# Key pace, softmax start, value pages and norm groups at other block numbers in a hybrid decoder layer

## What is computed

```python
h = rmsnorm(x); proj = h @ w_in                       # 2048 -> 13344 columns
q, k, v, z, xbc, dt, g_attn, g_ssm = split(proj)
attn = moba_attention(q, k, v)      # 16 heads of 64; own block of 256 and the best 3 past ones
ssm  = mamba2(z, xbc, dt)           # conv of width 4, SSD in chunks of 128, grouped RMS norm
merged = sigmoid(g_attn) * (attn @ w_attn_out) + sigmoid(g_ssm) * (ssm @ w_ssm_out)
x = x + rmsnorm(merged @ w_out)
x = x + rmsnorm(swiglu(rmsnorm(x)))                   # 2048 -> 5632 -> 2048
```

## Time and profile before

| | |
|---|---|
| median of three runs | 1809.43 us |
| profiled execution | 1807.29 us, span 1805.5 |
| mean granted TensorE clock | 0.995 of full |
| PE / VectorE / ScalarE / GpSimd busy | 99% / 66% / 51% / 12% |
| VectorE busy, 350 to 420 us | 65.6 of 70 us |
| VectorE busy, 690 to 760 us | 54.0 of 70 us |

### The profile page before, as it was taken

How to read it: one execution, slowest core, us unless ns; L and a number is a source line. 1 busy time by engine, 2 the same in 40 slices (tenths; PEclk the granted TensorE clock), 3 DMA queues, 4 the chain that set the end, 5 groups by cost and what they waited for, 6 DMA issues and landing times.

```text
span 1805.5 us, 35392 instructions
## 1 busy us (share of the span) xinstructions
PE 1782.1 (99%) x14613; PEld 1719.1 (95%) x14613; DVE 1195.2 (66%) x1666; ACT 918.3 (51%) x1737; POOL 216.2 (12%) x127
## 2 busy tenths in 40 slices
PE   8999999999999999999999999999999999999997
PEld 8999999998988988889999899999999999999997
DVE  6478999999887557745744666666666666444443
ACT  5544556554766557533444655554545454444342
POOL 2145644564000000000000000000000000000000
PEclk9999999999999999999999999999999999999998
DMA  8589987897789999695564387767777775655552
GB/s 253 177 272 330 320 265 261 278 305 235 222 281 317 303 295 344 217 304 177 180 223 155 116 281 221 225 226 231 230 217 232 229 235 182 216 176 170 175 180 80
DMA packets 397810, 421.40 MB, mean 233 GB/s; under 512 B 13033, under 2 KB 375465, under 8 KB 396585
## 3 DMA queue, kind: packets, MB, share of 16 engines
q10 hardware_dynamic: 284336, 285.35, 49.5%
q1 hardware_dynamic: 112960, 133.11, 22.6%
q0 software_dynamic: 352, 0.67, 0.2%
HBM read 400.70 MB, written 18.66 MB: 232 GB/s over the span
## 4 chain that ended last, share of the span: by engine, by line
PE 87%; DVE 8%; ACT 2%; issue 2%; DMA 0%; ACTq 0%; DVEq 0%; SPq 0%; POOL 0%; POOLq 0%
PE gemm L1733 27%; PE gemm L1734 27%; PE gemm L1735 26%; DVE w_lo L1197 3%; PE side L1985 2%; PE side L1695 1%; DVE conv_out L1189 1%; ACT w_hi L770 1%; DVE sc_flat L1391 1%; PE side L1696 1%; DMA xtok<-in_x_prompt 0%; DVE dec L1186 0%; DVE u L1189 0%; ACT dec L770 0%; PE side L1881 0%
## 5 line engine op out<-in xcount | busy, mean ns | idle before, releaser
L1197 DVE TENSOR_TENSOR w_lo<-raw,w_hi 128x1024 fp32r<-128x1024 f32 (+1 forms) x562 | 737.2, 1315 | 559.2 <-ACT w_hi L770 558.0
L1733 PE MATMUL gemm<-x_hi,w_hi 128*128 128x264 f32 x3312 | 953.1, 288 | 4.9 <-DVE w_lo L1197 3.1
L1735 PE MATMUL gemm<-x_hi,w_lo 128*128 128x264 f32 x3312 | 938.1, 283 | 0.0
L1734 PE MATMUL gemm<-x_lo,w_hi 128*128 128x264 f32 x3312 | 938.0, 283 | 0.0
L770 ACT ACTIVATE w_hi<-raw 128x1024 fp32r<-128x1024 f32 (+1 forms) x562 | 585.9, 1045 | 675.9 <-PE gemm L1735 674.3
L1733 PEld LDWEIGHTS gemm<-x_hi,w_hi 128*128 128x128 f32 x3312 | 623.6, 188 | 34.1 <-issue 25.7
L1734 PEld LDWEIGHTS gemm<-x_lo,w_hi 128*128 128x128 f32 x3312 | 624.4, 189 | 0.9 <-issue 0.5
L1735 PEld LDWEIGHTS gemm<-x_hi,w_lo 128*128 128x128 f32 x3312 | 621.1, 188 | 0.0
L1734 PE MATMUL gemm<-g_lo,w_hi 128*128 128x264 f32 x704 | 200.4, 285 | 0.0
L1733 PE MATMUL gemm<-g_hi,w_hi 128*128 128x264 f32 x704 | 200.1, 284 | 0.0
L740 POOL TENSOR_TENSOR kv<-kv,qb 128x1024 f32<-128x1024 f32 x64 | 177.4, 2780 | 185.1 <-DMA kv<-in_cache_k 185.1
(11 more groups left out here) (309 smaller groups left out, 1425.9 us busy)
## 6 DMA issues: line engine op xcount, KB each, us to landing
raw<-in_w_in ACTq DMA_DIRECT2D x99, 1024.0 KB, 7.0
raw<-in_w_gate ACTq DMA_DIRECT2D x44, 1024.0 KB, 5.2
raw<-in_w_up ACTq DMA_DIRECT2D x44, 1024.0 KB, 5.7
raw<-in_w_down ACTq DMA_DIRECT2D x40, 1024.0 KB, 5.3
kv<-in_cache_k SPq DMA_DIRECT2D x64, 512.0 KB, 5.5
kv<-in_cache_v SPq DMA_DIRECT2D x64, 512.0 KB, 5.9
st<-in_state_ssm SPq DMA_DIRECT2D x64, 256.0 KB, 5.3
raw<-in_w_ssm_out ACTq DMA_DIRECT2D x16, 1024.0 KB, 7.2
```

Of the source, the lines that this page charges most:

```text
L1197: v.tensor_tensor(w_lo[:, s, 0:blk.kts, cols], raw[:, s, 0:blk.kts, cols], w_hi[:, b % RING, 0:blk.kts].bitcast(fp32), ALU.subtract).then_ ...
L1733: mm(out, w_hi[:, b % RING, k], pr.hi[:, x], start=(x == 0), stop=False)
L1734: mm(out, w_hi[:, b % RING, k], pr.lo[:, x], start=False, stop=False)
L1735: ins = mm(out, w_lo[:, s, k, cols], pr.hi[:, x], start=False, stop=(x == pr.kt - 1))
```

## The change

The pace of the keys is 1.61 blocks a page instead of 1.58: the last page is multiplied at block 131 instead of 129. The softmax starts at 132 instead of 130; of its steps, TensorE's spreading of own_p is at SEL + 19 instead of + 20 (151, before 150), own_t at SEL + 23 instead of + 24 (155, before 154). The value pages of the four pairs start at 154, 175, 196, 218 instead of 152, 174, 196, 218. The norm groups 2 and 4 to 7 move forward by one, one, one, two and two blocks.

```diff
-K_PACE = 1.58
+K_PACE = 1.61
...
-        SEL = 130
+        SEL = 132
         CT_AT = 214
-        VG = [152 + 22 * w for w in range(4)]
-        UN = [196, 198, 200, 201, 203, 205, 207, 208]
+        VG = [154 + 21 * w for w in range(3)] + [218]
+        UN = [196, 198, 199, 201, 202, 204, 205, 206]
...
-                if b == SEL + 24:
+                if b == SEL + 23:
                     dve.wait_ge(sm_pe, 6)
                     dve.wait_ge(smp_cp, 3)
                     mul(own_t[:, :], smp[:, 2, :], side[3][:, 0:64])\
...
-                if b == SEL + 20:
+                if b == SEL + 19:
                     pe.wait_ge(p_done, 1)
```

## The result

The changed kernel takes 1812.32 us (median of 20 runs, 1808.84 to 1818.84), the one before 1809.35 in the same comparison (20 runs, 1805.69 to 1811.77). The ratio is 1.0019 with a 95% interval of 1.0011 to 1.0026: slower by 3.0 us, inside the 3.6 us that I counted as no change, 1.5 above the forecast of 1810.8. The profiled execution took 1813.73 (span 1811.9), 6.4 more than the one before.

What follows compares the result with a forecast made beforehand. TensorE, busy 99% of the span, bounds the kernel, so only its stops (6.6 us of interest) can be gained. Parts +0.3, +1.1 and 0 sum to +1.4 us on the median 1809.43: 1810.8, range 1806.0 to 1815.0.

Steps and rivals of the forecast that it cites:

- Part 1, transposes and own_t: New PE stops behind blocks 140 (1.2 us) and 148 (0.8), own_t's 1.7 gone: sum +0.3, bounds -1.7 to +2.0.
- Part 1, what own_t stood for: PE's block 152 waits 1.7 us for own_t; one block of distance becomes two, so the stop goes.
- Part 2, the first softmax product: PE's block 132 waits for reduction 63 under DVE's block 133: new stop 1.1 us, bounds 0.3 to 1.9.
- Part 2, the stops before blocks 121 and 126: PE's w_lo stops, with issue, 3.1 us together, stay as before; bounds -3.1 to +2.1.
- Part 3, the norm: x_lo waits in block 210 (1.0 and 0.8 us), none in 212: new 1.8, old 1.8, sum 0.
- A: Rival, faster: stops before 121 and 126 vanish, margins at 140 and 148 hold; 1805.7 us or less; chance 0.16.
- B: Rival, slower: a multiply holds up w_lo at DVE's blocks 130 to 133, one more near 121; 1814.5 us; chance 0.20.
- C: Rival: own_t is late at 155, its wait stays; +1.7, 1812.5 us; counted in no change, 0.64 with the forecast.

Runs made afterwards that it cites:

- short multiplies: GpSimd's multiplies of key pages 40 to 63 cut to 16 columns: 1805.79 us on the changed kernel, 1803.56 on the kernel before.
- halves: Every key multiply cut in two instructions of 512 columns: 1807.24 us on the changed kernel, 1803.45 with only values moved, 1804.76 on the kernel before.
- the late own_t: Kernel before with the product own_t done seven times on DVE, the first six without use: 1812.69 us against 1810.12, ratio 1.0009.

## Why the prediction came out as it did

It was forecast as no change within 3.6 us, and 1.5 of the 3.0 were missing. By its steps:

- **Part 1, transposes and own_t: right.** Forecast +1.2, +0.8, -1.7; after shows waits of 1.1, 0.5 and none for own_t. The reduction behind 140 ended in the order that I gave it, convolution and y sum first. own_t ended at 536.3 and PE took it at 538.1: 1.8 of margin, forecast 2. The part by itself: ratio 1.0000.
- **Part 1, what own_t stood for: incomplete.** I took its 1.7 as a distance of two blocks in the order. With short multiplies it goes with no block moved, and it goes when only the values move, for 1807.5. Moving the softmax added two waits that buy nothing.
- **Part 2, the first softmax product: at its upper value.** I took 1.1 between 0.3 and 1.9; it was 1.9 after, 1.3 and 1.4 in the versions without the norm groups and with the early qb transfer, 0.8 with halves, none with short multiplies. The path was the one that I wrote: multiply 63 runs from 443.91 to 446.32 over the w_lo at 444.61, which takes 2.79 in place of 1.22. The row of the w_lo held 3.31, and the rule of the Trainium skill that the prediction cites, both spoke for the upper end; taking the middle cost 0.8.
- **Part 2, the stops before blocks 121 and 126: the step that failed.** "From block 102 to 126 the new schedule is the old one with one key page less done [...] and I leave the 3.1 us in." Neither half of this holds. By `K_AT`, one multiply between blocks 102 and 126 does move: the one at block 109 is now at 108, with its load and its reduction one block earlier too. And the meetings are others. The stop before 121 grew by 1.85 and the two smaller ones shrank by 1.2, so +0.7 net; that and the 0.8 of above are the missing 1.5. GpSimd's multiply and DVE's w_lo of blocks 110 to 112 before:

```profile
367.83 3.45 POOL L740 TENSOR_TENSOR kv<-kv,qb 128x1024 f32<-128x1024 f32 x1 [0.60 <-DMA kv<-in_cache_k]
...
367.80 1.23 DVE L1197 TENSOR_TENSOR w_lo<-raw,w_hi 128x1024 fp32r<-128x1024 f32 x1 [0.27 <-ACT w_hi L770]
371.10 1.26 DVE L1197 TENSOR_TENSOR w_lo<-raw,w_hi 128x1024 fp32r<-128x1024 f32 x1 [2.08 <-ACT w_hi L770]
372.28 1.21 DVE L1391 TENSOR_REDUCE sc_flat<-kv 128x16 f32<-128x1024 f32 x1
374.13 2.15 DVE L1197 TENSOR_TENSOR w_lo<-raw,w_hi 128x1024 fp32r<-128x1024 f32 x1 [0.64 <-ACT w_hi L770]
```

and the same after:

```profile
368.39 2.40 POOL L740 TENSOR_TENSOR kv<-kv,qb 128x1024 f32<-128x1024 f32 x1
...
368.64 3.22 DVE L1197 TENSOR_TENSOR w_lo<-raw,w_hi 128x1024 fp32r<-128x1024 f32 x1
371.79 1.21 DVE L1391 TENSOR_REDUCE sc_flat<-kv 128x16 f32<-128x1024 f32 x1
372.92 6.20 DVE L1197 TENSOR_TENSOR w_lo<-raw,w_hi 128x1024 fp32r<-128x1024 f32 x2
```

It is the start that decides. Before, w_lo starts 0.03 us ahead of the multiply: it takes 1.23, and the multiply is the one that waits (3.45 in place of 2.4). After, the multiply starts 0.25 ahead, and w_lo takes 3.22. Before, DVE still finds 3.0 us of idle time here and has caught up. After, three w_lo in a row are held, and from here DVE has no idle time up to the stop: the w_lo of block 116 is ready 2.8 us before TensorE starts the block, against 5.2 before. (The moved reduction shows in these rows, behind the w_lo of 110 instead of 111.) What DVE carries reaches block 121 as another held w_lo:

```profile
411.05 1.20 DVE L1391 TENSOR_REDUCE sc_flat<-kv 128x16 f32<-128x1024 f32 x1
412.18 3.03 DVE L1197 TENSOR_TENSOR w_lo<-raw,w_hi 128x1024 fp32r<-128x1024 f32 x1
```

It is ready at 415.20 where PE wanted it at 411.7, 3.5 earlier. In the version without the norm groups, which has the same key schedule, the w_lo of blocks 109 to 116 are as far ahead as in the softmax version at the old pace (within 0.1 us). So the moved page alone doesn't make the arrears. There they come from one meeting between the w_lo of 116 and 117. DVE's two small products there, then GpSimd, first at the old pace:

```profile
392.27 0.76 DVE L1189 SCALAR_TENSOR_TENSOR bct<-conv_th,conv_out 128x264 f32<-128x264 f32 x2
392.95 1.21 DVE L1197 TENSOR_TENSOR w_lo<-raw,w_hi 128x1024 fp32r<-128x1024 f32 x1
...
393.12 3.32 POOL L740 TENSOR_TENSOR kv<-kv,qb 128x1024 f32<-128x1024 f32 x1 [5.85 <-DMA kv<-in_cache_k]
```

and then at the new one:

```profile
393.85 2.94 DVE L1189 SCALAR_TENSOR_TENSOR bct<-conv_th,conv_out 128x264 f32<-128x264 f32 x2
...
394.11 2.38 POOL L740 TENSOR_TENSOR kv<-kv,qb 128x1024 f32<-128x1024 f32 x1 [5.27 <-DMA kv<-in_cache_k]
```

At the old pace the multiply comes 0.85 after the start of these products, when the w_lo of 117 is under way, and waits itself (3.32). At the new one it comes at 0.26 and keeps the second product out for 2.2 us; the w_lo of 117 is ready 3.7 us ahead instead of 5.9, and the stop is 3.7 instead of 1.7. The sum of what multiplies hold up doesn't tell this: over the w_lo of blocks 26 to 133 it is 59.4 us before and 61.3 after. Both multiplies were released by the transfer of their page, so a page that lands 0.6 us earlier or later can be worth 2 us of stop. What made it land then isn't shown, nor why all three profiles at a pace of 1.61 with whole multiplies end at 3.5 to 3.7 here, while of five at 1.58 four have 1.7 and one 0.1. The transfer of qb, which I had named, isn't it.
- **Part 3, the norm: right.** 1.2 and 0.7 in block 210 for the forecast 1.0 and 0.8, none in 212; ratio 1.0000 alone.
- **Not foreseen: the clock.** No term of the sum had it. It makes the profiled execution 3.0 us slower, and the medians by between nothing and 1, as said above.
- **The rivals.** A didn't come: only the two smaller stops shrank, by 1.2, and the one before 121 grew. B's mechanism came in two versions at the old pace, before block 130 (1.3 in the softmax alone, 1.3 with the late own_t), and in the changed kernel as the upper value at L1954 and the meeting before 121. C didn't come.
- **A reading.** The 0.30 in the row of w_hi is how long ScalarE had been idle, not the time since PE's release. Nothing in the sum hangs on it.

The sum with measured stops: part 1 -0.1 by the waits, +0.5 by the block starts (138 to 195); part 2 +1.9, +0.7 and up to 0.3 in restarts; part 3 +0.1. That is 2.6 to 3.5, without anything for the clock, and 3.0 was measured.

## What to carry to other kernels

When two engines shut each other out, the same order of work gives no promise of the same stops (the kernel with the norm groups alone is the one before up to block 196, and has 0.1 before block 121 for 1.7): a forecast over such a stretch needs a range for every stop in it, and an experiment that makes the one side short shows what all meetings together cost. Cutting the instruction that holds the other engine in two is worth more than moving the work around (5 us for one edit here, while a softmax and a norm that moved gained nothing, values that moved gained 2, and a pace lost 3). Before a chain of steps is moved to remove a wait, ask for the smallest move that removes it: the values alone did it here.

## What the runs showed of the hardware

- A DVE product with two SBUF inputs is kept out until the running GpSimd multiply ends, even one of 128x16 (2.27 us for 0.18). The one that starts first wins: with w_lo 0.03 us ahead it was the multiply that took 3.45. Reductions of a whole page, with one input, stayed at 1.21. Nor were DVE's products of the convolution held up, which read TensorE's sum in PSUM (conv_out from gemm): in the trace before, 50 that started inside a multiply took 0.462 to 0.474, and 42 clear of one 0.465 to 0.475.
- A GpSimd product of 512 columns took 1.69 and one of 256 columns 1.01 in place of 2.78 for 1024, meetings included: a page costs 3.4 or 4.0, so pieces aren't free for GpSimd.
- Stops of PE of 1.8, 1.9, 3.3, 3.5, 3.6 and 3.7 were followed by half clock for 3.4 us, once 6.8 (behind the 3.3); stops of 1.7 were not (before block 121 in four profiles, for own_t in two), nor 1.3 and 1.4 at the first softmax product. These are the rows, and no rule is drawn from them. A stop of 3.5 us therefore costs 5 where the clock falls.
- Behind block 289, where PE has many short products and transposes, seven of the fourteen profiles show 3.4 or 6.8 us at half clock and seven none: 1 to 2.3 us in one profiled execution. It doesn't follow what was changed near block 120; the seven are among the eight profiles taken last (short multiplies, halves, and all after them), and the first six have none, so it may go with when a run was made. What decides it isn't shown. It is reason enough to read a change of this size from the stops and the median, and not from two spans.
